# A third of the modulation products stays on TensorE, two thirds are summed on VectorE

## The reference

```python
# block 1 (block 2: c_2, w_ada_2, b_ada_2)
mod = silu(c) @ w_mod + b_mod               # (1, 1024) @ (1024, 6144)
sh1, sc1, g1, sh2, sc2, g2 = split(mod, 6)
mc  = split(silu(c_ctx) @ w_mod + b_mod, 6) # only mc[0], mc[1] are used
h   = rms_norm(x, norm1_w) * (1 + sc1) + sh1
hc  = rms_norm(ctx, norm1_w) * (1 + mc[1]) + mc[0]
...                                          # retention and Fourier branch of h
y   = (g_r * (ret @ w_ret_out) + g_f * (four @ w_four_out)) @ w_out
x   = x + g1 * y
h2  = rms_norm(x, norm2_w) * (1 + sc2) + sh2
u   = depthwise_conv3(h2 @ w_up, conv_w, conv_b); a, val = split(u, 2)
x   = x + g2 * ((gelu(a) * val) @ w_down)
```

## Time and profile before

| | before |
|---|---|
| median of three runs | 2573.54 us |
| lowest, highest | 2570.39, 2577.47 us |
| the profiled execution | 2578.59 us |
| its span | 2576.8 us |
| mean granted TensorE clock | 0.969 of full speed |
| TensorE busy | 2384.9 us |
| VectorE busy | 778.3 us |
| ScalarE busy | 628.7 us |
| GpSimd busy | 128.5 us |

### The profile page before, as it was taken

The page is one execution under the profiler, slowest core; times in us unless marked ns, Lnnn a source line. Parts: engine busy times, 40 slices in busy tenths (PEclk is TensorE's granted clock), DMA queues, the critical chain, the costliest instruction groups (busy, mean ns, idle before and its releaser), DMA issues.

```text
span 2576.8 us, 26206 instructions
## 1 busy us (share of the span) xinstructions
PE 2384.9 (93%) x11440; PEld 1540.6 (60%) x11440; DVE 778.3 (30%) x1015; ACT 628.7 (24%) x891; POOL 128.5 (5%) x128
## 2 busy tenths in 40 slices
PE   5999999999999998999999998998989898898988
PEld 3774767677777787877667787443333434343434
DVE  4427412344453524454652433010101010000102
ACT  5205213234233324532552321000000000000001
POOL 0113000011000001120000011000000000000000
PEclk7999999999999999999999998999999999999998
DMA  7210233542545323221001234799999999999994
GB/s 262 98 54 24 86 110 126 204 163 98 196 150 178 134 97 131 98 74 66 1 1 66 98 122 182 310 428 427 428 428 427 428 427 427 428 427 428 427 428 185
DMA packets 116824, 571.51 MB, mean 222 GB/s; under 512 B 5390, under 2 KB 28215, under 8 KB 92007
## 3 DMA queue, kind: packets, MB, share of 16 engines
q1 hardware_dynamic: 115104, 565.58, 54.7%
q0 software_dynamic: 1200, 4.13, 0.5%
q10 hardware_dynamic: 407, 0.13, 0.0%
HBM read 567.73 MB, written 2.10 MB: 221 GB/s over the span
## 4 chain that ended last, share of the span: by engine, by line
PE 72%; DMA 21%; DVE 3%; ACT 2%; issue 1%; POOL 0%; ACTq 0%; SPq 0%; DVEq 0%; POOLq 0%
PE ps L737 42%; DMA arena<-in_w_exp_up 9%; PE ps L1257 8%; DMA arena<-in_w_exp_gate 6%; PE ps L1320 5%; DMA arena<-in_w_exp_down 3%; PE ps L1240 2%; DMA weights<-in_w_exp_gate 2%; PE ps L830 1%; PE ps L1143 1%; PE ps L1161 1%; PE ps L1019 1%; PE ps L1101 1%; PE ps L971 1%; PE ps L1272 1%
## 5 line engine op out<-in xcount | busy, mean ns | idle before, releaser
L737 PE MATMUL ps<-weights_r 128*128 128x512 f32 (+1 forms) x2784 | 865.9, 391 | 19.6 <-DVE hT_r L1853 7.4
L737 PEld LDWEIGHTS ps<-weights_r 128*128 128x128 f32 x2784 | 523.6, 190 | 143.8 <-issue 36.6
L737 PE MATMUL ps<-hT_r,weights_r 128*128 128x512 f32 x1264 | 466.3, 393 | 6.4 <-DVE arena L1955 6.4
L1257 PE MATMUL ps<-weights,arena 128*64 128x512 f32 x768 | 351.9, 615 | 63.9 <-DMA weights<-in_w_exp_up 49.7
L1259 PE MATMUL ps<-weights,arena 128*64 128x512 f32 x768 | 352.7, 616 | 0.0
L1846 DVE TENSOR_TENSOR weights_r<-weights,weights_r 128x4096 fp32r<-128x4096 f32 (+1 forms) x47 | 201.6, 4289 | 428.8 <-ACT weights_r L1405 426.8
L1257 PEld LDWEIGHTS ps<-weights,arena 128*64 128x64 f32 x768 | 105.5, 141 | 291.0 <-issue 289.1
L737 PEld LDWEIGHTS ps<-hT_r,weights_r 128*128 128x128 f32 x1264 | 240.1, 190 | 60.4 <-issue 11.0
L1405 ACT ACTIVATE weights_r<-weights 128x4096 fp32r<-128x4096 f32 (+1 forms) x47 | 165.3, 3517 | 339.2 <-PE ps L737 139.0
L737 PE MATMUL ps<-arena_r,weights_r 128*128 128x512 f32 (+1 forms) x640 | 229.5, 395 | 3.5 <-DVE mod_cols L1861 3.5
L1320 PE MATMUL ps<-weights,hT 128*64 128x512 f32 x384 | 169.8, 598 | 3.3 <-DMA weights<-in_w_exp_down 3.3
(11 more groups left out here) (278 smaller groups left out, 2425.7 us busy)
## 6 DMA issues: line engine op xcount, KB each, us to landing
weights<-in_w_exp_gate SPq DMA_DIRECT2D x48, 2048.0 KB, 23.3
weights<-in_w_exp_up SPq DMA_DIRECT2D x48, 2048.0 KB, 26.4
weights<-in_w_exp_down SPq DMA_DIRECT2D x48, 2048.0 KB, 28.2
weights<-in_w_in SPq DMA_DIRECT2D x18, 2048.0 KB, 8.3
arena<-in_w_exp_gate SPq DMA_DIRECT2D x16, 2048.0 KB, 27.0
arena<-in_w_exp_up SPq DMA_DIRECT2D x16, 2048.0 KB, 28.2
arena<-in_w_exp_down SPq DMA_DIRECT2D x16, 2048.0 KB, 29.2
weights<-in_w_mod SPq DMA_DIRECT2D x12, 2048.0 KB, 7.9
```

Source lines behind the costliest of these rows:

```text
L737: last = pe.matmul(t, a if w_first else b, b if w_first else a, start=(k == 0 and n == 0), stop=(k == kt - 1 and n == len(pairs) - 1))
L1257: la = pe.matmul(bank(b0 + n)[0:64, :], xe[:, 2 * j + r, 0:64], wa[:, r, n * 512:(n + 1) * 512], start=start, stop=stop)
```

## The change

Chunks 4 to 11 of both modulations, 16 of 24, are no longer multiplied on TensorE. VectorE sums them over the eight feature tiles, with silu(c) as the scalar of each partition (`mod_sum`: one tensor_scalar and seven linked scalar_tensor_tensor of 128x512); for these chunks the context vector is left out. TensorE's turn then multiplies by a column of ones and so adds up the partitions (4 matmuls, one column each). ScalarE no longer copies them. The slot of such a chunk is spent when its sum is made (`mod_summed`).

The order changes too. Block 1's chunk 4 is loaded ahead of `in1` 6, chunk 5 ahead of the DFT matrices, chunk 6 behind them; 7 to 10 stand behind the four gate groups; the four projection groups have none behind them; 11 stands behind the first half of `out1`, and mod2 0 behind its second. The step of mod2 0 moves from the middle of `out1` to before its last tile. In the up stage chunk j's sum is made in two halves, behind the conv pairs of tiles 1 and 2, and the rest of the next weights moves from before the conv pair of tile 0 to behind it.

The diff, cut to its core:

```diff
+PE_MODS = 4
...
     def merge(tag):
...
-            if tag == "m1":
-                mod_step("mod1", 4 + i, 4)
-        if tag == "m1":
-            b.add(("mod1", "T", 11), "D")
+            if tag == "m1" and i < 5:
+                b.add(("mod1", "T", 6 + i), "D")
...
         mod1(3)
-        for i in range(1, 7):
+        for i in range(1, 6):
             in1(i)
+        mod1(4)
+        in1(6)
+        mod1(5)
         chunk("dft", dft_len)
+        mod1(6)
         for i, (kind, part, nq) in enumerate(MERGE):
...
-            mod1(4 + i)
+            if kind == "gate":
+                mod1(7 + i)
...
         for nq in range(2):
             chunk(("out1", nq), kmaj(w_out[0], 512 * nq, 512 * nq + 512))
-            if nq == 0:
-                mod2(0)
+            (mod1 if nq == 0 else mod2)(11 if nq == 0 else 0)
...
         def wait_spent(sp, n):
 
-            if order[n] in last_tile:
+            if order[n][0] in ("mod1", "mod2") and order[n][1] >= PE_MODS:
+                sp.wait_ge(S["mod_summed"], summed_mods(*order[n]))
+            elif order[n] in last_tile:
...
-        m_sbs = [at(5632, 2, L), at(9216, 2, L), at(16384, 2, L)]
+        m_sbs = [at(5632, 2, L), at(4096, 2, L), at(16384, 2, L)]
...
             def mod_turn(tag, c):
 
+                if c >= PE_MODS:
+                    pe.wait_ge(S["mod_summed"], summed_mods(tag, c))
+                    t = claim(pe, (tag, "T", c))
+                    for j in range(4):
+                        last = pe.matmul(t[:, j:j + 1], m_sb(tag, c)[:, j * P:(j + 1) * P], const("one"),
+                                         start=True, stop=True)
+                    fill((tag, "T", c), last)
+                    return
...
+            def mod_step(tag, c):
+
+
+                if c:
                     mod_turn(tag, c - 1)
+                if c >= PE_MODS:
+                    return
...
-                    if tag == "m1":
-                        mod_step("mod1", 4 + i, 4)
-                if tag == "m1":
-                    mod_turn("mod1", 11)
+                    if tag == "m1" and i < 5:
+                        mod_turn("mod1", 6 + i)
...
                 if tag == "out1":
-                    pe.wait_ge(S["silu_ready"], 4)
-                    mod_step("mod2", 0, 0)
+                    mod_turn("mod1", 11)
...
                 for n in range(4, KT):
                     feature_tiles((tag, 1), [(tag, n)], x, c0=n % 4 * P)
+                    if tag == "out1" and n == 6:
+                        pe.wait_ge(S["silu_ready"], 4)
+                        mod_step("mod2", 0)
...
             token_tiles(("in1", 6), [("f", t) for t in range(TT)], h_parts)
+            mod_turn("mod1", 4)
...
+            mod_turn("mod1", 5)
             pe.wait_ge(S["dist_in"], 48)
...
             merge_gates("m1", 0)
-            wait_full(act_e, ("mod1", 11))
+            prepare(("out1", 0))
+            act_e.wait_ge(S["mod_summed"], summed_mods("mod1", 11))
             mod_silu(3)
-            prepare(("out1", 0))
-            mod_rows("mod2", 0)
             prepare(("out1", 1))
-            norm_squares(2, "n2", xT, L, lambda k: wait_freed(act_e, ("out1", k)))
+            norm_squares(2, "n2", xT, L, lambda k: wait_freed(act_e, ("out1", k)),
+                         between=lambda: mod_rows("mod2", 0))
...
-                mod_rows("mod2", j + 1)
+                if j + 1 < PE_MODS:
+                    mod_rows("mod2", j + 1)
...
+            def mod_sum(tag, c, ks=range(KT)):
+
+                w = slot(landed(ve, (tag, c)), KT)
+                acc = m_sb(tag, c)
+                for k in ks:
+                    if k == 0:
+                        ve.wait_ge(S["silu_ready"], 2 if tag == "mod1" else 4)
+                        if c >= 2 and (tag, c) not in (("mod1", 4), ("mod1", 5)):
+                            wait_full(ve, (tag, "T", c - 2))
+                        last = ve.tensor_scalar(acc, w[:, 0, :], sc_pad[:, 0, 0:1], None, ALU.mult)
+                    else:
+                        last = ve.scalar_tensor_tensor(acc, w[:, k, :], sc_pad[:, k, 0:1], acc, ALU.mult, ALU.add)
+                    if k < KT - 1:
+                        link(last)
+                    else:
+                        last.then_inc(S["mod_summed"], 1)
...
                     if tag == "m1":
-                        prepare(("mod1", 4 + i))
-                        if i:
-                            mod_columns("mod1", 3 + i)
+                        if i < 4:
+                            mod_sum("mod1", 7 + i)
+                        if i < 5:
+                            mod_columns("mod1", 6 + i)
+                        if i == 4:
+                            mod_scales("mod1", (2,))
                 if tag == "m1":
-                    mod_columns("mod1", 11)
-                    mod_scales("mod1", (2,))
+                    mod_sum("mod1", 11)
...
+                if n == 4:
+                    mod_sum("mod1", 4)
             prepare(("in1", 6))
+            mod_sum("mod1", 5)
+            mod_columns("mod1", 4)
             prepare("dft")
+            mod_sum("mod1", 6)
+            mod_columns("mod1", 5)
...
             for j in range(UPN):
-                prepare(("up", j))
                 for n in range(4):
...
+                    if n == 0:
+                        prepare(("up", j))
+                    elif n < 3 and j + 1 >= PE_MODS:
+                        mod_sum("mod2", j + 1, range(4 * n - 4, 4 * n))
...
-            wait_full(po, ("mod2", 11))
+            wait_full(po, ("mod2", "T", 11))
...
+    put("one", 1.0)
```

More of the change, by code:

```diff
@@ L69 @@
 for _name, _w in (("ident", 128), ("swap1", 128), ("swap2", 128), ("mask", 256), ("iota", 64),
-                  ("age", 4), ("modsel", 2), ("slotcol", 1)):
+                  ("age", 4), ("modsel", 2), ("slotcol", 1), ("one", 1)):
     CONST[_name] = (_n, _n + _w)
@@ L143, in norm @@
         b.add((tag, "wide"), "D")
-    def mod_step(tag, c, first):
-        if c > first:
+    def mod_step(tag, c):
+        if c:
             b.add((tag, "T", c - 1), "D")
-        b.add((tag, c), "A")
+        if c < PE_MODS:
+            b.add((tag, c), "A")
     def merge(tag):
@@ L164, in rope @@
                 b.add((tag, "swap", i - 1), "D")
-    mod_step("mod1", 0, 0)
+    mod_step("mod1", 0)
     b.add(("n1", "wide"), "D")
     for c in range(1, 4):
-        mod_step("mod1", c, 0)
+        mod_step("mod1", c)
     b.add(("mod1", "T", 3), "D")
@@ L205, in plan_banks @@
         b.add(("f", t), "A")
+    b.add(("mod1", "T", 4), "D")
     for g in range(FG):
@@ L208, in plan_banks @@
             b.add(("fa", g, m), "A")
+    b.add(("mod1", "T", 5), "D")
     for g in range(FG):
@@ L214, in plan_banks @@
         if n == 3:
-            mod_step("mod2", 0, 0)
+            b.add(("mod1", "T", 11), "D")
+        if n == 6:
+            mod_step("mod2", 0)
     norm("n2")
@@ L219, in plan_banks @@
             b.add(("up", j, n), "D")
-        mod_step("mod2", j + 1, 0)
+        mod_step("mod2", j + 1)
     b.add(("mod2", "T", 11), "D")
@@ L336, in build_two_blocks @@
             wsel_ready xe_full xe_low xe_high gate_full up_full silu_done hm_ready hmt_full hmt_ready y_ready sc_full x_added
-            stored decay_exp stage2_in""".split()
+            stored decay_exp stage2_in mod_summed""".split()
         S = {n: es.enter_context(nc.semaphore(n)) for n in names}
@@ L493, in build_two_blocks, with summed_mods @@
             last_tile["up", j] = ("up", j, 3)
+        def summed_mods(tag, c):
+            return c - PE_MODS + 1 + (12 - PE_MODS if tag == "mod2" else 0)
         def wait_spent(sp, n):
-            if order[n] in last_tile:
+            if order[n][0] in ("mod1", "mod2") and order[n][1] >= PE_MODS:
+                sp.wait_ge(S["mod_summed"], summed_mods(*order[n]))
+            elif order[n] in last_tile:
                 sp.wait_ge(S["tile_full"], banks.where[last_tile[order[n]]] + 1)
@@ L1457, in merge_gates @@
                             A(h_high[:, k, :], merge_views[tag][0][:, k, :], ACT.Copy).then_inc(S["merged_high"], 1)
-                    if tag == "m1":
-                        mod_rows("mod1", 4 + i)
             rows = [
@@ L1860, in mod_columns @@
                 b = cols[:, vi, V1["b_mod"] + 4 * c:V1["b_mod"] + 4 * c + 4]
+                if c >= PE_MODS:
+                    free((tag, "T", c), "D", ve.tensor_tensor(cc[:, 4 * c:4 * c + 4, 0], t[:, 0:4], b, ALU.add))
+                    return
                 free((tag, "T", c), "D", ve.tensor_tensor(
@@ L1983, in projected @@
                 if tag == "out1":
-                    prepare(("mod2", 0))
+                    mod_columns("mod1", 11)
                 else:
```

## The result

| | before | after |
|---|---|---|
| median, all runs so far | 2574.8 us (6 runs, 2570.39 to 2578.19) | 2586.95 us (6 runs, 2581.62 to 2589.69) |
| the profiled execution, its span | 2578.59, 2576.8 us | 2587.07, 2585.3 us |
| mean granted TensorE clock | 0.969 | 0.961 |

The ratio of the times is 1.0045, with a 95% interval of 1.003 to 1.006: the change makes the kernel slower by 12 us. The forecast was 2579.3 us, with a range of 2560 to 2592 and no measurable difference as the likeliest outcome.

What follows compares the result with a forecast made beforehand. TensorE, busy 93% of the span, was taken as the bound, replaced from up chunk 3 by a loop through VectorE, DMA queue and ScalarE. Terms: -20.4 + 2.0 + 24.2 = +5.8 on the median 2573.54, giving 2579.3 us; range 2560 to 2592.

Steps and rivals of the forecast that it cites:

- the mechanism that was called decisive: Up stage from chunk 3: a loop through VectorE, DMA queue and ScalarE takes TensorE's place, 27.3 us a chunk, 24.2 lost.
- Merge stage: Block 1: retention weights ready at 469.7 against 484.35, 14.6 us gained; output projection at 515.3 against 539.58, 24.3 gained.
- Here some is given back.: End of merge: late up 0 load delays the squares, GpSimd's adds end about 567.4; the stage's gain is 20.4 us.
- Up stage, chunk 0.: VectorE's rest of the next weights, behind its first conv pair, ends at 625.0 where TensorE wants it at 622.99: 2.0 lost.
- The paragraph on the clock: TensorE's gaps may lower its clock, 2.6 us more: no cost in the up loop, already paid at the start of down.
- This is the step that decides.: Up stage from chunk 3: w_up's slot now waits for VectorE's sum; rounds of 27.3 us, 226.8 against 202.6, 24.2 lost.
- D: Start of VectorE's first conv pair in up chunk j; the sum is done at D + 14.7, next D 27.3 us later.
- The first D: Up stage: 15.4 us from the chunk's start to VectorE's first conv pair, with w_up's rounding starting 11.0 in, then 3.63, 0.7.
- The last chunk.: End of up stage: four pairs 5.8, rest 4.3, sum 6.0 and a tail of 4.2, together 20.3 us.
- Rival 1: Up stage: sums are covered or the load is early, chunks take 22.82 us, time 2546 us; chance 0.13.
- Rivals 2 and 3: VectorE's added operation: at 921 ns, 2588.8 us, chance 0.20; or nearer 0.64, 2573 us (2565 with better-covered norm), chance 0.10.
- Rival 4: Merge stage: retention weights still late as sum 10 waits behind other VectorE work; up to 8 us, 2587; inside forecast's range.

Runs made afterwards that it cites:

- the kernel with the rest first: The change with only the rest of the next weights back ahead of the first conv pair, sum halves left between the pairs: 2577.95 us, 1.0014 of before.
- the up part alone: The kernel before with block 2's chunks 4 to 11 summed in the up stage as in the change, block 1 untouched: 2602.69 us, 1.011 of before.
- the sum stands twice in the loop: The change with both halves of each block 2 sum computed twice, first into a row nothing reads: 2633.83 us, 1.0226 of before.
- the kernel with the sum first: The change with VectorE's whole sum first in each up chunk, then the rest of the next weights, then the conv pairs: 2545.01 us, 0.9888 of before.

## Why the prediction was right, and what it missed

The time lies in the range, and the mechanism that was called decisive is the one that decides. The likeliest outcome, no measurable difference, did not come: 12 us slower, where the sum had 5.8. Point by point:

- **"Merge stage", gates and retention weights.** Forecast 469.7 for the retention group, 469.52 measured; 515.3 for the output projection, 514.74 measured. The gain is 24.8 us, 24.3 forecast, and TensorE's own relief, eight products of 1.85 or 14.8 us, is only part of it. That 469.7 was hit to 0.2 is in part luck: it was the forecast end of the weights' rest, with TensorE ready at 468.8. The rest ended at 468.6, and TensorE came at 469.5, since 48 matmuls behind the short wait at 445 took 12.79 us in place of 11.0. The hole of before was read as lasting from 464.24 to 484.35; it was 6.4 us. The sum used only the second of these times, so nothing in it moves.
- **"Here some is given back."** GpSimd's adds end at 567.08, forecast 567.4. But the norm matmuls behind them were costed at the duration of before, 1.93, and took 3.56, the next ones 2.09 in place of 1.62: the granted clock was 0.73 in that stretch, and TensorE had been idle for 5.6 us. Up 0 came at 577.2 and not at 575.3. This is the first missed term, 1.9.
- **"Up stage, chunk 0."** 2.0 lost, as forecast, within 0.3. Behind the 2 us of waiting the clock was at 0.72 for the first six us of chunk 1, whose group took 23.66 in place of 22.03: 1.6 missed. The paragraph on the clock looked at the loop, where it costs nothing, and at the start of down, and not at the edges, where TensorE is the bound.
- **"This is the step that decides."** The sum at D + 14.7: 14.66 measured. The added operation: 0.79 from start to start, as taken; it stands in no row of before, and the nearest row was the right one, not the 921 ns one. The kernel before also has 22 two-input operations of this shape with all operands in SBUF at a mean of 688 ns (L2121), so the shape alone does not give 921. The round: 27.3 forecast, 27.2 in four of seven, 26.8 in the last, 28.3 and 28.5 in two. In those two the chain shows loads of 8.9 and 9.1 in place of 7.7. Seven rounds took 192.4 in place of 191.1. Why two loads were slower was not tried and stays open; one such load is in the kernel with the rest first, one in the up part alone, and none where the sum stands twice in the loop. TensorE's idle time was forecast as 4 to 5 us in each chunk and was 1.6 to 5.6, by the clock of the group before.
- **The first D** came 16.0 after the chunk's start, not 15.4.
- **The last chunk.** 20.3 forecast, 20.34 measured (866.07 to 886.41).

So 1.9 + 0.3 + 1.6 + 0.6 + 1.3 is 5.7, the whole difference between 880.7 and 886.41. No step of the sum failed; its terms left out the clock at two edges of the stage and the spread of the loads. The other 2 us between 2579.3 and 2586.95 are scatter: behind the start of down the changed kernel's profiled execution is 3.0 shorter in the same code, and that of before lay 5.0 above the median that the forecast was set on.

Rival 1 (sums covered, chunks of 22.8, 2546 us) is not what the change does, but it is what the kernel with the sum first does, at 2545. Rivals 2 and 3 fell with their prices, 0.92 and 0.64, against 0.76. Rival 4 fell with the retention group at 469.5.

The rule quoted from the Trainium skill (VectorE: DVE Perf Modes, The TRN2 errata), an estimate of 0.59 us for the operation, is not borne out: 0.76 each here. The one on the clock gate (TensorE: Matmul & The Clock Gate, HAM oscillation) is, in part: the first six us behind the waits of 3.6, 4.4 and 5.6 in the up stage had a granted clock of 0.52, 0.50 and 0.59, those behind the waits of 1.6 and 2.6 had 1.00, with no effect on the loop.

## What to carry to other kernels

When work moves from the engine that is the bound to one that is mostly idle, ask what the work releases: here the release of a weight slot moved with it, from the end of a product to the end of a sum that itself stood behind instructions waiting for the next weights. Write down the loop of waits round by round and add it up; if it comes out longer than the bound engine's round, the place of the new work in its engine's order matters more than its amount (here 42 us between two orders of the same instructions). Then look at the edges of the stage, where here a wait of 2 us was followed by a slower group.

## What the runs showed of the hardware

- A scalar_tensor_tensor of 128x512 with everything in SBUF took 0.76 us (0.75 with a PSUM operand), and the next one that waited for it started 0.79 after it; one that did not wait started 0.66 or 0.67 after it. Eight linked operations took 6.0 us.
- After some waits TensorE's granted clock was at the lower level for part of the work that followed: behind 5.6 us, 16 matmuls of one column took 3.56 us, where they took 1.93 behind 1.4; behind 2.1 us a group of 96 took 23.66 in place of 22.03. Behind waits of 1.6 and 2.6 us in the up stage it was at full speed. What decides between them no run here shows.
- The two 1 MB loads of a w_up chunk, issued 0.4 us apart with nothing ahead of them, were ready for ScalarE 8.2 us after the first issue in most rounds, and 1.1 to 1.3 later in two.
